# A hybrid attention layer on one core: probabilities scaled three slots ahead, a dilation-4 exchange by fixed 0/1 matrices and a pick, and loads in another order

## The chip, the cores and the metric

One Trainium2 chip, one of its cores. The metric is the device time of the whole kernel in microseconds, the median of several runs; lower is better.

## The reference

One decoder layer on x of 4096 tokens by 1024, in float32. The normed input goes through one projection whose columns feed three head groups; each group's output is gated by SiLU, all go through one output projection, are normed and added to x.

```python
qa, ka, va, ga, qb, kb, vb, gb, qc, gc = jnp.split(proj, IN_SPLITS, axis=-1)
oa, _ = banded_attention(qa * scale, ka, va, A_WINDOW - 1, sink)       # A: 6 heads, 2 key heads, window 128
for (win, dil) in ((128, 1), (512, 4), (2048, 16)):                    # B: 6 heads
    o, lse = banded_attention(to_strided(qb * scale, dil)[:, :, :, None, :],
                              to_strided(kb, dil), to_strided(vb, dil), win // dil, None)
    outs.append(from_strided(o[:, :, :, 0], B, dil)); lses.append(from_strided(lse[..., 0], B, dil))
wts = jax.nn.softmax(jnp.stack(lses, axis=0), axis=0)
ob = jnp.sum(wts[..., None] * jnp.stack(outs, axis=0), axis=0)
pc = jax.nn.softmax(jnp.einsum('bshd,bmhd->bhsm', qc * scale, mk), axis=-1)   # C: 4 heads, 256 memory tokens
y = jnp.concatenate([oa * silu(ga), ob * silu(gb), oc * silu(gc)], axis=-1)
h = h + rms_norm(jnp.einsum('bse,ed->bsd', y, w_out), post_norm)
```

## The kernel before

Three stages follow each other: `project_stage` (to about 1192 us of the profile), `attend_stage` (to about 2190) and `finish_stage`. The change is in the attention stage alone, in `head_group` and `attend_stage`.

**Units, slots and rounds.** The sequence is cut in two halves of 2048 tokens. A *phase* is one head on one half: 12 phases of group B, then 12 of A, then 8 of C. The work of a phase is a list of *units* (128 queries against 128 or 256 keys), 48 in B (16 for each dilation) and 16 in A and C, taken in pairs: `NP` is 24 or 8. In B the units come dilation 16 first, then in two groups with dilations 4 and 1.

The engines are driven by *rounds*. In round r the scores of phase r are made (`a`), while phase r-1 (`c`) is turned and multiplied with the values, and what is left of phase r-2 (`b`) is finished. A round has as many *slots* as the phase has pairs. `TAIL` says how many pairs of a phase are left for the round after the next: 8 in B, 2 in A and C. `slots_of` writes the table, so that the pair worked on in slot i of a round is `b`'s for i below the tail, then `c`'s.

Each slot does, on each engine in this order:

- **PE** (`tensor_round`): `scores` of the new pair (two products per unit, L952 and L953, since keys are held as a high and a low part), `turn` of the current pair's probabilities by transposing (L1017, into `ps_t`), `exchange`, and in every other slot `times_values` of two pairs (L1001). The scores have three PSUM buffers (`NS`).
- **DVE** (`vector_round`): `exchange`, `scale` of the pair of the next slot by its weight (L1135), `finish` of a bank of outputs (L1164 adds it to what was kept, L1169 multiplies by the gate), and the masked minimum of the scores, `scores` (L1048).
- **ACT** (`scalar_round`): `copy` of the turned pair to SBUF (L1207), `keep`, the exponentials with their sums (L1183), `exchange`.

**The exchange.** In B the minima and sums (`stat`) of the dilations 16 and 4 are held by strided queries and must be brought to the order of dilation 1, where the three are combined, and the weights (`work[:, 7]`) must go back. This is done by PE with 0/1 matrices: DVE first multiplies `stat` with a small 0/1 table `sel`, spreading it into `moved` (L1087 for dilation 16, 128 columns; L1090 for dilation 4, 512 columns), in slots 1 and 2. PE multiplies in slot 3 (L961, L965: `moved` as the stationary side, `sel` as the moving). DVE and ACT form the weights in slots 4 and 5 (L1096 to L1113), DVE spreads them (L1117, L1120), PE multiplies in slot 6 (L970, L972), and DVE copies them to `coef` in slot 7 (L1125).

**SyncE's queue.** `loads` issues all loads of a group, head after head, each behind the waits that free its buffer; a wait holds all that stands behind it:

```python
load_q(h, 0)                      # scores 8 slots into the phase before, and its queries copied
if not first: load_gate(h - 1, 1) # y_stored: output of two rounds ago stored
if new_keys: scored(*early_of, ...); load_k(h, 0)   # B: 13 slots into phase (h-1, 1)
if new_keys: scored(p1, NP, total); load_k(h, 1)
load_q(h, 1); load_gate(h, 0)
if new_keys: valued(*early_of, early); load_v(h, 0)
if new_keys: valued(p1, NP, total); load_v(h, 1)    # all values of phase (h-1, 1) done
```

In group A new keys and values come with heads 0 and 3 alone. **GpSimd** (`moves`) copies each phase's queries into two more orders (`spread_queries`, L601 four times and L609) once the phase before has its scores, and then issues the store of an output (L1228).

## Time and profile before

| | us |
|---|---|
| runs, median of 3 (2553.11 to 2563.31) | 2553.58 |
| profiled execution, its own time | 2546.56 |
| its span | 2545.1 |
| PE busy | 2283.6 (90%) |
| DVE busy | 1343.6 (53%) |
| ACT busy | 1141.8 (45%) |
| POOL busy | 134.5 (5%) |
| mean granted clock of TensorE | 0.947 |

The profiled execution is one run, 7.0 us below the median. Busy shares are over the whole span. A PE instruction counts as busy until its modelled end, so neighbours overlap. The clock is given as a share of 2.4 GHz; it is 1.0 or 0.5 at any time, and a mean between them tells how long it was at either. "L1017 <- DVE L1135" reads: the instruction of line 1017 waited, and that of line 1135 on DVE ended the wait.

### The profile page before, as it was taken

To read this page: it belongs to the slowest core of one execution; us is meant where nothing else is said; L and a number is where in the kernel's file an instruction comes from. 1 tells how busy PE (TensorE), PEld (TensorE's weight loads), DVE (VectorE), ACT (ScalarE), POOL (GpSimd) and SP (SyncE) were. 2 spreads that over 40 slices of the span, in tenths; PEclk is the share of its full clock that TensorE was granted. 3 is DMA by queue.
4 is the path that set the end of the run, shared out by engine and by line. 5 is a ranking of instruction groups with operands and counts; after the bars stand their busy time and mean duration, and the time that the engine had idled before them with its cause. 6 is when DMAs were issued, how large, how long until landed. Compare 5 with 4: busy or idle time off the path is not lost. (4 is left out here: it accounts for less than half of the span.)

```text
span 2545.1 us, 43938 instructions
## 1 busy us (share of the span) xinstructions
PE 2283.6 (90%) x13740; PEld 1912.2 (75%) x13740; DVE 1343.6 (53%) x3975; ACT 1141.8 (45%) x2967; POOL 134.5 (5%) x158
## 2 busy tenths in 40 slices
PE   5999999999999999998888798888877678799998
PEld 4887788877887788877777687776666567588887
DVE  4651347223751357212787777877787767333333
ACT  4123531245223532223777666765576667322221
POOL 0000000000000000010110101010121201000000
PEclk9999999999999999998799889998998889899999
DMA  5346334553345333474646737557368655344443
GB/s 183 136 165 165 129 112 148 176 146 117 132 172 162 129 124 141 138 213 114 113 83 134 142 67 149 107 110 143 84 137 177 147 144 154 120 149 148 142 139 114
DMA packets 349590, 350.27 MB, mean 138 GB/s; under 512 B 151568, under 2 KB 278160, under 8 KB 345360
## 3 DMA queue, kind: packets, MB, share of 16 engines
q1 hardware_dynamic: 341872, 322.54, 46.9%
q0 software_dynamic: 7584, 26.22, 4.1%
q8 instruction: 50, 0.82, 0.1%
q14 instruction: 84, 0.69, 0.1%
HBM read 222.07 MB, written 126.62 MB: 137 GB/s over the span
## 5 line engine op out<-in xcount | busy, mean ns | idle before, releaser
L58 PE MATMUL p_ps<-p_uT_hi,p_w_hi 128*128 128x512 f32 x1536 | 603.0, 393 | 2.1 <-DVE p_w_lo L389 2.1
L60 PE MATMUL p_ps<-p_uT_hi,p_w_lo 128*128 128x512 f32 x1536 | 599.4, 390 | 0.0
L59 PE MATMUL p_ps<-p_uT_lo,p_w_hi 128*128 128x512 f32 x1536 | 599.2, 390 | 0.0
L1183 ACT ACTIVATE probs<-probs,a_stat 128x256 f32<-128x256 f32 (+1 forms) x896 | 434.8, 492 | 107.3 <-DVE a_stat L1048 105.2
L952 PE MATMUL a_ps_s<-k_hi,q 128*128 128x256 f32 (+1 forms) x896 | 299.9, 352 | 98.5 <-DMA k_lo<-scratch_qk_lo 37.3
L1017 PE MATMUL a_ps_t<-a_ident,probs 128*128 128x128 f32 x1660 | 277.4, 291 | 70.5 <-DVE probs L1135 68.7
L58 PEld LDWEIGHTS p_ps<-p_uT_hi,p_w_hi 128*128 128x128 f32 x1536 | 289.4, 188 | 62.1 <-issue 2.5
L60 PEld LDWEIGHTS p_ps<-p_uT_hi,p_w_lo 128*128 128x128 f32 x1536 | 289.1, 188 | 60.9
L59 PEld LDWEIGHTS p_ps<-p_uT_lo,p_w_hi 128*128 128x128 f32 x1536 | 289.2, 188 | 59.0
L389 DVE TENSOR_TENSOR p_w_lo<-p_w_raw,p_w_hi 128x1024 fp32r<-128x1024 f32 x96 | 117.6, 1225 | 391.5 <-ACT p_w_hi L286 373.0
L1048 DVE CUSTOM_DVE_ANT_0 probs<-a_ps_s,a_maskB 128x256 f32<-128x256 f32 (+1 forms) x704 | 251.2, 395 | 134.0 <-PE a_ps_s L953 129.7
L1207 ACT ACTIVATE a_pT<-a_ps_t 128x512 f32<-128x512 f32 (+1 forms) x412 | 232.6, 567 | 193.7 <-PE a_ps_t L1017 193.4
L1135 DVE TENSOR_SCALAR probs<-probs,a_coef 128x256 f32<-128x256 f32 (+1 forms) x896 | 290.5, 369 | 26.8 <-issue 25.7
L952 PEld LDWEIGHTS a_ps_s<-k_hi,q 128*128 128x128 f32 x896 | 187.8, 210 | 142.9 <-issue 117.4
L1017 PEld LDWEIGHTS a_ps_t<-a_ident,probs 128*128 128x128 f32 x1660 | 204.1, 149 | 88.3 <-DVE probs L1135 81.8
L1001 PE MATMUL a_ps_o<-a_pT,a_v 128*64 128x128 f32 x3320 | 265.2, 301 | 2.9 <-ACT a_pT L1207 1.4
L953 PE MATMUL a_ps_s<-k_lo,q 128*128 128x256 f32 (+1 forms) x896 | 261.5, 308 | 0.0
L1001 PEld LDWEIGHTS a_ps_o<-a_pT,a_v 128*64 128x64 f32 x3320 | 199.9, 148 | 50.4 <-issue 31.7
L58 PE MATMUL f_ps<-f_w_hi,f_y_hi 128*128 128x512 f32 x512 | 200.3, 391 | 18.0 <-DVE f_w_lo L1538 18.0
L324 ACT ACTIVATE p_o_hi<-p_rot 128x512 fp32r<-128x512 f32 x80 | 50.6, 632 | 358.4 <-DVE p_rot L450 358.4
L59 PE MATMUL f_ps<-f_w_lo,f_y_hi 128*128 128x512 f32 x512 | 200.1, 391 | 0.0
L60 PE MATMUL f_ps<-f_w_hi,f_y_lo 128*128 128x512 f32 x512 | 200.0, 391 | 0.0
(113 smaller groups left out, 2371.6 us busy)
## 6 DMA issues: line engine op xcount, KB each, us to landing
p_w_raw<-in_w_in SPq DMA_DIRECT2D x96, 512.0 KB, 3.9
scratch_qk_hi<-p_o_hi SPq DMA_DIRECT2D x96, 256.0 KB, 2.0
scratch_qk_lo<-p_o_lo SPq DMA_DIRECT2D x96, 256.0 KB, 2.4
a_v<-scratch_v SPq DMA_DIRECT2D x40, 512.0 KB, 6.2
p_x<-in_x SPq DMA_DIRECT2D x32, 512.0 KB, 4.2
scratch_v<-p_o_v SPq DMA_DIRECT2D x256, 64.0 KB, 2.0
scratch_gate<-p_rot SPq DMA_DIRECT2D x64, 256.0 KB, 2.2
a_gate<-scratch_gate SPq DMA_DIRECT2D x64, 256.0 KB, 4.3
```

Of the source, the lines that this page charges most:

```text
L58: nc.tensor.matmul(out, w_hi, m_hi, start=first, stop=False)
L59: nc.tensor.matmul(out, w_hi, m_lo, start=False, stop=False)
L60: return nc.tensor.matmul(out, w_lo, m_hi, start=False, stop=last)
L389: nc.vector.tensor_tensor(w_lo[:, b, :, :].rearrange("p k n -> p (k n)"), w_raw[:, b, :], w_hi[:, b, :, :].rearrange("p k n -> p (k n)").b ...
L952: nc.tensor.matmul(out, w, keys_of(k_hi[:, 0:NKEY], u), start=True, stop=False)
L953: last = nc.tensor.matmul(out, w, keys_of(k_lo[:, 0:NKEY], u), start=False, stop=True)
L1001: last = nc.tensor.matmul(place_of(ps_o[j * HD:(j + 1) * HD, bank % 2, :], u), v[name][:, half, tile, :], pT[:, e % 4, j, at * P:(at + 1) ...
L1017: last = nc.tensor.transpose(ps_t[:, e % 2, j, at * P:(at + 1) * P], probs[:, s, 2 * e + j, at * P:(at + 1) * P], ident[:])
L1048: last = nc.vector.tensor_tensor_reduce(out=probs[:, s, 2 * slot + j, a:], in0=ps_s[:, slot % NS, j, a:], in1=masks[u.kind][:, a:], scale= ...
L1135: last = nc.vector.tensor_scalar(place, place, coef[:, s, u.column:u.column + 1], None, ALU.mult)
L1183: last = nc.scalar.activation(place, place, ACT.Exp, scale=-1.0, bias=stat[:, s, 0, u.column:u.column + 1], accum_out=stat[:, s, 1, u.colu ...
L1207: nc.scalar.activation(pT[:, e % 4, :, a[0]:], ps_t[:, e % 2, :, a[0]:], ACT.Copy).then_inc(turned_copied, 1)
```

## The change

1. `TAIL` goes from 8 to 12 in B and from 2 to 4 in A and C. DVE scales the pair that is turned three slots later. In a slot of DVE the order is now: exchange (A and C), scale, scores, finish, a new part `gated`, exchange (B). `gated` is the product with the gate, split off from `finish` and one slot later.
2. The dilation-4 part of the exchange has no spreading. `sel` holds, beside the small tables, four fixed 128x128 0/1 matrices `group4` (540 columns instead of 60). PE multiplies `stat` with them directly, 32 columns a product, four products instead of eight; DVE then picks from the result with a product with `col4` and a sum (into `picked` and back to PSUM). On the way back it is four products and the same pick. `moved` shrinks. The steps move: DVE in slots 1, 3, 5, 7, PE in slots 2 and 6, the end of a slot on DVE instead of its start.
3. `loads` is written out for all heads without a hardware loop, in another order. The second value load of a head now follows the next head's first query load and, in B, its first key load. In A and C the next head's first key load follows the gate load.
4. Group C's keys lie in the place of `v4`, its values in that of `v16`.
5. `start` of the score table at a switch of groups is max(0, lag - NP + 1) instead of 2.

GpSimd still copies the queries.

```diff
-    TAIL = 8 if kind == "B" else 2
+    TAIL = 12 if kind == "B" else 4
...
+    if kind == "C":
+        k_hi, k_lo = (buf.v["v4"][:, i, :, :].rearrange("p t n -> p (t n)")[:, 0:2 * NMEM].bitcast(F32R) for i in range(2))
+        v = {"v1": v["v16"]}
...
+        load_q(0, 0)
+        load_k(0, 0)
+        if prev:
+            load_mask()
+        for h in range(heads):
+            if new_keys(h):
                 load_k(h, 1)
-            if not prev and first:
-                load_v(h, 0)
+            if not prev and h == 0:
+                load_v(0, 0)
             load_q(h, 1)
             load_gate(h, 0)
-            if new_keys and (prev or not first):
-                valued(*early_of, early)
+            if new_keys(h) and (prev or h > 0):
                 load_v(h, 0)
-            if new_keys:
-                valued(p1, NP, total)
+            if h + 1 < heads:
+                load_q(h + 1, 0)
+            if new_keys(h + 1) and kind == "B":
+                load_k(h + 1, 0)
+            if new_keys(h):
                 load_v(h, 1)
+            load_gate(h, 1)
+            if new_keys(h + 1) and kind != "B":
+                load_k(h + 1, 0)
...
-            if kind == "B" and slot == 3:
-                pe.wait_ge(spread, 2 * p + 2)
+            if kind == "B" and slot == 2:
+                pe.wait_ge(spread, p + 1)
                 for x in range(2):
-                    nc.tensor.matmul(ps_x[:, 16 * x:16 * x + 16], moved[:, x, 0, :], col16,
-                                     start=True, stop=True)
-                    for c in range(NCH):
-                        at = 32 + 16 * x + 4 * c
-                        last = nc.tensor.matmul(ps_x[:, at:at + 4], moved[:, x, 1 + c, :], col4,
-                                                start=True, stop=True)
+                    nc.tensor.matmul(ps_x[:, 16 * x:16 * x + 16], moved[:, x, :], col16, start=True, stop=True)
+                for b in range(NCH):
+                    last = nc.tensor.matmul(ps_x[:, 128 + 32 * b:160 + 32 * b].rearrange("p (x n) -> p x n", x=2), group4[:, b, :],
+                                            stat[:, s, :, 16:32], start=True, stop=True)
                 last.then_inc(gathered, 1)
...
-            if slot == 4:
+            if slot == 1:
+                dve.wait_ge(sums_ready, p * NP + NP)
+                nc.vector.tensor_tensor(moved[:, 0:2, :].rearrange("p x (r a) -> p x r a", a=8),
+                                        stat[:, s, :, 0:16].unsqueeze(3).broadcast_to([P, 2, 16, 8]),
+                                        sel16.unsqueeze(1).unsqueeze(1).broadcast_to([P, 2, 16, 8]), ALU.mult).then_inc(spread, 1)
+            if slot == 3:
                 dve.wait_ge(gathered, p + 1)
+                own(nc.vector.tensor_tensor(picked[:, 0:128].rearrange("p (n r) -> p n r", r=NCH),
+                                            ps_x[:, 128:256].rearrange("p (n r) -> p n r", r=NCH),
+                                            col4.unsqueeze(1).broadcast_to([P, 32, NCH]), ALU.mult))
+                own(nc.vector.reduce_sum(ps_x[:, 32:64].rearrange("p (n b) -> p b n", b=NCH),
+                                         picked[:, 0:128].rearrange("p (b n r) -> p b n r", b=NCH, r=NCH),
+                                         mybir.AxisListType.X))
...
-            start = 2 if a and a.g is not c.g else 0
+            start = max(0, lag - a.g.NP + 1) if a and b and a.g is not b.g else 0
...
-                if c:
+                if c and c.g.kind != "B":
                     c.parts.exchange(c.phase, i)
-                if slot.next:
-                    x, e = slot.next
+                if slot.ahead:
+                    x, e = slot.ahead
                     x.parts.scale(x.phase, e)
+                for v in slot.new:
+                    a.parts.scores(a.phase, v)
                 if slot.two_before:
                     x, e = slot.two_before
                     x.parts.finish(x.phase, e)
-                for v in slot.new:
-                    a.parts.scores(a.phase, v)
+                if slot.three_before:
+                    x, e = slot.three_before
+                    x.parts.gated(x.phase, e)
+                if c and c.g.kind == "B":
+                    c.parts.exchange(c.phase, i)
```

**SyncE's queue in group B**, from the second value load of a head to the next head's first keys; before (the last value load ahead of the loop over heads, then the loop's first loads; `a_v` are the values, "ISA" carries a wait):

```order
L842 DMA a_v<-scratch_v 128x16x64 [waits B_values_done]
L842 DMA a_v<-scratch_v 128x16x64 x2
...
L812 DMA q<-scratch_qk_hi 64x2048
L813 DMA q<-scratch_qk_lo 64x2048
...
L854 DMA a_gate<-scratch_gate 64x16x64
...
L831 ISA [waits B_scores_ready]
L831 DMA k_hi<-scratch_qk_hi 64x16x128 x2
L831 DMA k_lo<-scratch_qk_lo 64x16x128 x2
```

And with the change, from a head's first value load to its second gate load:

```order
L855 DMA a_v<-scratch_v 128x16x64 [waits B_values_done]
L855 DMA a_v<-scratch_v 128x16x64 x2
L813 DMA q<-scratch_qk_hi 64x2048 [waits e_q_copied,B_scores_ready]
L814 DMA q<-scratch_qk_lo 64x2048
L839 DMA k_hi<-scratch_qk_hi 64x16x128 [waits B_scores_ready]
L839 DMA k_hi<-scratch_qk_hi 64x16x128
L839 DMA k_lo<-scratch_qk_lo 64x16x128 x2
L855 DMA a_v<-scratch_v 128x16x64 [waits B_values_done]
L855 DMA a_v<-scratch_v 128x16x64 x2
L863 DMA a_gate<-scratch_gate 64x16x64 [waits B_y_stored1]
L863 DMA a_gate<-scratch_gate 64x16x64
```

The keys stood behind both value loads, the queries and the gate; now they stand ahead of the second value load and of the gate.

**DVE in group B, slot 1 of an odd round, before** (L1087 and L1090 spread the minima, L1164 sums a bank):

```order
L1087 TENSOR_TENSOR a_moved<-a_stat,a_sel 128x128 [waits B_sums_ready]
L1090 TENSOR_TENSOR a_moved<-a_stat,a_sel 128x512
L1135 TENSOR_SCALAR probs<-probs,a_coef 128x256 x2
L1147 REGISTER_ALU
L1164 TENSOR_TENSOR probs<-a_ps_o,probs 64x2x128 [waits B_kept,B_y_ready,B_y_free_gate_loaded1,B_values_done]
L1164 TENSOR_TENSOR probs<-a_ps_o,probs 64x2x128 x3
L1168 REGISTER_ALU
L1169 TENSOR_TENSOR a_gate<-probs,a_gate 128x16x32 [waits B_bank_read]
```

**With the change, slot 5 of such a round** (L1025 is the minimum, L1141 the sum of a bank, L1079 the first step of the weights, L1091 the last; L1112 is the scaling of the next slot):

```order
L1025 ISA a_stat 128x1
...
L1141 TENSOR_TENSOR probs<-a_ps_o,probs 64x2x128 [waits B_kept,B_y_ready,B_y_free_gate_loaded1,B_values_done]
L1141 TENSOR_TENSOR probs<-a_ps_o,probs 64x2x128 x3
L1079 TENSOR_TENSOR a_work<-a_work,a_ps_s 128x32 [waits B_exps_ready]
L1081 TENSOR_TENSOR a_work<-a_work,a_stat 128x16
...
L1091 TENSOR_TENSOR a_moved<-a_work,a_sel 128x128 [waits B_shifted]
L1112 TENSOR_SCALAR probs<-probs,a_coef 128x256 x2
```

The exchange stood ahead of the slot's scaling; it is now the slot's last work, behind the minimum and, in slot 5, behind the sum of a bank. `B_spread_back` follows L1091.

**PE at the first exchange, before** (slot 3):

```order
L1017 MATMUL a_ps_t<-a_ident,probs 128x128 x3
L959 ISA
L961 MATMUL a_ps_s<-a_sel,a_moved 128x16 [waits B_spread]
L965 MATMUL a_ps_s<-a_sel,a_moved 128x4 x4
L961 MATMUL a_ps_s<-a_sel,a_moved 128x16
L965 MATMUL a_ps_s<-a_sel,a_moved 128x4 x4
```

**With the change** (slot 2; the line ahead is the turn of that slot):

```order
L994 MATMUL a_ps_t<-a_ident,probs 128x128 [waits B_turned_copied,B_weighted]
L994 MATMUL a_ps_t<-a_ident,probs 128x128 x3
L940 MATMUL a_ps_s<-a_sel,a_moved 128x16 [waits B_spread]
L940 MATMUL a_ps_s<-a_sel,a_moved 128x16
L942 MATMUL a_ps_s<-a_stat,a_sel 128x32 x4
```

Eight products of four columns became four of 32, one slot earlier.

## Rows read from the trace of the kernel before

**Rows 1.** The page: the span, then busy time and share of each engine
```profile
span 2545.1 us, 43938 instructions
...
PE 2283.6 (90%) x13740; PEld 1912.2 (75%) x13740; DVE 1343.6 (53%) x3975; ACT 1141.8 (45%) x2967; POOL 134.5 (5%) x158
```

**Rows 2.** Windows A:B: length, then busy us of PE, PEld, DVE, ACT, POOL; granted clock; DMA share; GB/s
```profile
40.00:1192.00 1152.00, 1111.82 (x5002) 913.48 (x5001) 462.00 (x694) 349.41 (x471) 11.85 (x15) 0.99 0.45 143
1255.00:1765.00 510.00, 437.82 (x3853) 377.86 (x3852) 392.35 (x1730) 355.56 (x1264) 60.66 (x71) 0.90 0.59 116
1765.00:1836.00 71.00, 57.79 (x522) 48.35 (x521) 46.80 (x169) 37.27 (x105) 7.07 (x6) 0.88 0.43 90
1836.00:2027.00 191.00, 138.82 (x1290) 119.10 (x1290) 142.78 (x536) 126.73 (x418) 35.98 (x34) 0.91 0.73 156
```

**Rows 3.** The same: group B's rounds 5 and 6, and a stretch of its round 1
```profile
1404.10:1458.60 54.50, 41.16 (x354) 34.60 (x352) 40.44 (x175) 37.25 (x135) 9.85 (x12) 0.90 0.78 147
1458.60:1507.30 48.70, 47.84 (x415) 42.20 (x415) 36.23 (x168) 33.32 (x117) 1.88 (x3) 0.83 0.38 76
1215.40:1235.90 20.50, 14.30 (x64) 13.70 (x64) 12.62 (x62) 11.36 (x46) 0.00 (x0) 0.50 0.13 31
```

**Rows 4.** Waits of PE, 1192 to 1765 us: us in total, times, longest
```profile
PE a_ps_t L1017 <- DVE probs L1135: 39.7, 35, 2.2
PE a_ps_s L952 <- DMA k_lo<-scratch_qk_lo: 23.8, 4, 6.7
...
PE a_ps_s L952 <- issue: 5.9, 1, 5.9
PE a_ps_s L961 <- DVE a_moved L1090: 5.2, 1, 5.2
PE a_ps_s L970 <- DVE a_moved L1120: 2.6, 1, 2.6
```

**Rows 5.** Timeline of SyncE's DMA issues in round 5 of B: start, length
```profile
1402.73 30.13 SPq L842 DMA_DIRECT2D a_v<-scratch_v  x6
...
1439.59 1.44 SPq L854 DMA_DIRECT2D a_gate<-scratch_gate  x2
1441.39 4.09 SPq L831 DMA_DIRECT2D k_hi<-scratch_qk_hi  x2
```

**Rows 6.** Timeline of DVE at the start of that round
```profile
1406.45 1.85 DVE L1087 TENSOR_TENSOR a_moved<-a_stat,a_sel 128x128 f32<-128x128 f32 x1
...
1409.35 1.72 DVE L1164 TENSOR_TENSOR probs<-a_ps_o,probs 64x256 f32<-64x256 f32 x4
```

**Rows 7.** Timeline of POOL in the same place
```profile
1403.91 2.40 POOL L601 CAST q<-q 128x512 fp32r<-128x512 f32 x4 [18.38 <-PE a_ps_s L953]
1406.26 1.89 POOL L609 CAST q<-q 128x2048 fp32r<-128x2048 f32 x1
```

**Rows 8.** Groups by line and shape, 1100 to 2250 us: busy, mean ns, idle before
```profile
L965 PE MATMUL a_ps_s<-a_sel,a_moved 128*128 128x4 f32 x192 | 29.4, 276 | 0.0
...
L1090 DVE TENSOR_TENSOR a_moved<-a_stat,a_sel 128x512 f32<-128x512 f32 x24 | 18.1, 753 | 0.0
...
L1087 DVE TENSOR_TENSOR a_moved<-a_stat,a_sel 128x128 f32<-128x128 f32 x24 | 14.7, 611 | 3.6 <-ACT probs L1183 3.6
```

**Rows 9.** Waits of PE in group A, 1836 to 2027 us
```profile
PE a_ps_t L1017 <- DVE probs L1135: 18.8, 13, 1.8
PE a_ps_s L952 <- DMA k_lo<-scratch_qk_lo: 13.4, 1, 13.4
PE a_ps_s L952 <- issue: 13.3, 1, 13.3
PE a_ps_s L952 <- POOL q L609: 9.0, 3, 4.6
```

**Rows 10.** Timeline of SyncE: the gate load ahead of A's second keys
```profile
1898.69 1.34 SPq L854 DMA_DIRECT2D a_gate<-scratch_gate  x2
```

**Rows 11.** Waits of PE in group C
```profile
PE a_ps_s L952 <- DMA k_lo<-scratch_mk_lo: 23.8, 3, 8.4
```

More of the change, by code:

```diff
@@ L969, in exchange @@
                 pe.wait_ge(spread_back, p + 1)
-                nc.tensor.matmul(ps_x[:, 64:80], moved_back[:, 0, :], col16, start=True, stop=True)
-                for c in range(NCH):
-                    last = nc.tensor.matmul(ps_x[:, 80 + 4 * c:84 + 4 * c], moved_back[:, 1 + c, :], col4,
+                nc.tensor.matmul(ps_x[:, 64:80], moved[:, 2, :], col16, start=True, stop=True)
+                for r in range(NCH):
+                    last = nc.tensor.matmul(ps_x[:, 256 + 16 * r:272 + 16 * r], group4[:, r, :], work[:, 7, 16:32],
                                             start=True, stop=True)
@@ L1312, in slots_of @@
             if not c:
-                return [named(new=[v], pair=None, before=None, two_before=None, next=None)
+                return [named(new=[v], pair=None, before=None, two_before=None, three_before=None, ahead=None)
                         for v in range(a.g.NP)]
```

138 lines of the change are left out of this document (54 added, 84 removed).

## The prediction, made before the kernel was run

> **What bounds the kernel now.** The page gives PE as busy for 90% of the span [rows 1], DVE for 53%; that is a mean over stages with different limits, so I read the windows by stage first. The projection stage (first row of [rows 2]) has PE busy for 1111.8 of 1152.0 us at a granted clock of 0.99: nothing that the diff touches could shorten it. Attention is the stretch with room. In 1255 to 1765 us, which is rounds 2 to 11 of head group B, PE is busy 437.8 of 510.0, DVE 392.4 and ACT 355.6, with the clock at 0.90. So ten rounds take 51.0 us each, no engine is full, and three engines each carry 36 to 44 us of every round. Such a stretch is bound by the waits among them, and by the clock.
>
> Next the same view for single rounds [rows 3]. Round 5 lasts 54.5 us with PE busy for 41.2; round 6 lasts 48.7 with PE busy for 47.8, but at a clock of 0.83. The odd round loses time in stands, the even one in half clock. A mean of 0.90 over 510 us means that a fifth of it ran at the lower level (1.2 instead of 2.4 GHz); were PE the bound all through, that would cost 0.10 x 510 = 51 us.
>
> The waits of PE [rows 4] then name the stands. There are two kinds: 39.7 us, 35 times, for DVE to scale the probabilities that PE transposes (L1017 waits for L1135), and 23.8 + 5.9 = 29.7 us, five times (the last is written "issue", at the switch to group A), for keys.
>
> Why are keys late? SyncE's queue shows it [rows 5]. In round 5 (from 1404.1) the six value loads stand ahead of everything. The second three of them waited for the values of the phase before the last, so that the row spans 30.1 us, to 1432.9. Then come the queries, the gate (1439.6), and only at 1441.4 the keys. PE starts on them at 1458.6 [rows 3]: 17.2 us after their first issue.
>
> Why is scaling late? DVE's timeline [rows 6]: one expansion of the exchange takes 1.85 us and the sum of a finished bank 1.72, both ahead of scaling that is done only one slot ahead of its use. The longest of PE's stands for it is 2.2 us [rows 4].
>
> **The change, part by part.** The sum is against the profiled execution, 2546.6 us (span 2545.1). It lies 7.0 us below the median of the runs, 2553.6; I add 7 at the end.
>
> *Keys of group B.* In the new queue the keys of the next head stand ahead of the second value load. They are released by slot 13 of 24 of an odd round: 13/24 x 43 us = 23 us into it, and 17.2 us more makes 40.5, inside a round of 42 to 43 us. Of the stands I take all: **-29.7**. The cover is thin: if a round shrinks below 40 us the keys bound it again. The value load that they pass is needed 12 slots into the next round, some 20 us later, so it costs nothing. The gate load moves behind both; its user is a finish at slot 5 of a later round, nothing again.
>
> *Scaling three slots ahead.* The turn of a pair then finds it scaled one or two slots earlier (a slot is 43/24 = 1.8 us), and the new order in a slot puts the minima before the sum of a bank. **-39.7** for the old stands. New ones appear. PE's exchange products now stand in slots 2 and 6, and each needs the work that DVE does last in the slot before. In slot 5 the sum of a bank, 1.72 us [rows 6], comes ahead of the exchange. For PE's stand there I bound 0 (no such stand in rounds 2 to 11) and 5.2 us (the longer of the two in round 1 [rows 4]); I take 2.0, near the 1.72 that is put in front. In slot 1 the GpSimd copies still run [rows 7]; the expansion under them took 1.85 us where its mean over all 24 is 0.61 [rows 8]. Between 0 and 1.85 I take 0.8. That is 2.8 x 10 rounds = **+28**.
>
> *Exchange.* Four of the eight dilation-4 products of the first step go. The 192 records of 29.4 us [rows 8] are 24 sets of four products (two records each), 1.2 us a set; of two sets a round one remains, with 32 columns instead of 4. I take 1.0 us a round: **-10**. The second step keeps its four products. On DVE the wide expansions of 0.75 us (L1090 twice [rows 8], and L1120, of the same size) go, three small products and sums come: some 1 us less a round. It is beside PE's work except in slots 1 and 5, where I have counted it.
>
> *Clock.* With keys and scaling on time the stands that precede the falls of the clock are gone, but the new ones at slots 2 and 6 are in their place. Of the 51 us I take two thirds, **-34**; the ends are 0 and -51.
>
> Rounds 2 to 11: -29.7 - 39.7 + 28 - 10 - 34 = **-85.4**, that is 42.5 us a round. PE's own need is (437.8 - 51)/10 = 38.7, DVE's 39.2, so 42.5 leaves each some 8% of slack, which is plausible for three engines coupled by double buffers.
>
> *The rest of attention.* Round 1: of 7.8 us at the exchange [rows 4] 5 go, as the wide expansions do: **-5**. Start: the constants table grows from 60 to 540 columns on the queue that PE waits for before its first scores: **+1**, by its size. Switch to A, 1765 to 1836 us: PE is idle for 13 us of that window [rows 2]; as it has no key load in it, I take 10 for stands for scaling, which go, and two more pairs with few scores beside them come: **-8**. Group A, 1836 to 2027: DVE is busy 142.8 of 191, PE 138.8. The 18.8 us of stands for scaling [rows 9] lie under DVE's own work, which keeps its order at slot 1: 0 for them. Of the 9.0 us for copied queries the longest, 4.6, comes from a query load behind a value load, which is now passed: **-4.6**. But the keys of A's second key head and C's first loads stand behind a gate load [rows 10], which needs the output of two rounds ago stored. With the tail at 4 slots instead of 2 that store comes two slots later; a slot of A is (191 - 27)/80 = 2 us (ten rounds of eight, less the two long stands), and this happens twice: **+8** on the 13.4 and 13.3. Group C: the same gate load still stands ahead of the keys; 23.8 us [rows 11] stay, as the store is two slots (3 us) later but no longer meets a query load. Its last round has two pairs more with nothing beside them: **+2.4**. Together: -5 + 1 - 8 - 4.6 + 8 + 2.4 = **-6.2**.
>
> Total: 2546.6 - 85.4 - 6.2 = 2455.0; with the 7 us to the median **2462**.
>
> **Two rules beside the rows.** The clock: [rows 3] show 0.83 in a round with under 1 us of idle PE that follows a 6.7 us stand, and 0.50 over 20.5 us in which PE was busy 14.3. The Trainium skill, "TensorE: Matmul & The Clock Gate", Part 1 and "HAM oscillation", says that the gate follows how busy the array has lately been, so that gaps are paid twice. By that rule alone, if the gaps vanish, all 51 us return and the sum is 2445. By the rows, gaps remain, hence two thirds.
>
> The copies: during the POOL copies the expansion took 1.85 us against a mean of 0.61 [rows 7, 8]. The Trainium skill, "SBUF — State Buffer", "Who interferes with whom", says that GpSimd and a DVE instruction with two SBUF inputs take the shared port pair in turn, the loser blocked for a whole instruction. This speaks against the change: the new expansion has two SBUF inputs, sits in slot 1 under the copies, and PE now waits for it one slot earlier.
>
> **The rivals.**
> - *Smoother*: DVE keeps ahead, as in the clean middle of a round, and PE never stands at slots 2 and 6. Then the 28 us are not paid and the clock returns in full (17 more): 2462 - 45 = **2417**. For it: no stand at the exchange in rounds 2 to 11 [rows 4]. Against: the bank's sum now ahead of it. 0.20.
> - *Copies at the exchange*: the copies of 2.40 + 1.89 us [rows 7] hold DVE up in slots 0 and 1; PE's stand in slot 2 grows by 2.7, to 3.5 us a round (+27), and the clock gives nothing back (+34): **2523**. 0.15.
> - *No gain*: the keys stay late, since another load of the queue (the first value load or the gate) waits longer with the tail of 12 slots, and new stands eat the rest: about **2550**. 0.05.
> - *Slower*: every round behaves like round 1 does now. There PE stands 5.2 + 2.6 us at the two exchanges and then has 20.5 us at half clock [rows 3, 4], 18 us in all. On 38.7 - 1 us of work that makes 56 us a round instead of 51: +50, with the +6 to +10 of the later stores some **2610**. It decides once PE's stands at slots 2 and 6 exceed about 7 us a round with the clock falling after each. In round 1 DVE is alone with the scores; later rounds gave PE other work in between. 0.04.
> - That the change doesn't do what it says: the order of instructions shows keys and scaling moved as told, so I give it nothing.
>
> **How the numbers follow.** The forecast has 0.56, with a range of its own of 2430 to 2495. With both neighbours the range 2412 to 2515 takes in the smoother case and the nearer part of the copies case, and leaves out the last two. About 0.5% (13 us) is what a measurement can tell from no change. Faster by more: 0.56 + 0.20 + 0.15 = 0.91; same 0.05; slower 0.04.
>
> **What would show it.** Right: the wait of PE for k_lo in group B gone; L1017's wait for scaling under 8 us in B; rounds of 41 to 44 us; a clock of 0.95 or more in B; waits of PE for the moved table at the first products of slots 2 and 6, 1 to 3 us a round; the 13 us stands in A and the 8 us ones in C still there or slightly longer. Wrong: a new wait for keys or values in B; a clock still at 0.90; stands at the exchange over 5 us; A rounds longer than 16.5 us because queries come late.

## The result, and the profile after

| | before | after |
|---|---|---|
| median of 20 runs each, us | 2554.39 | 2561.97 |
| lowest to highest | 2548.15 to 2563.80 | 2554.82 to 2567.41 |
| ratio, 95% interval | | 1.0025 (1.0015 to 1.0035) |
| profiled execution, own time (span), us | 2546.6 (2545.1) | 2561.1 (2559.3) |

The changed kernel is 0.25% slower, within the 0.5% that the prediction calls no change, and 100 us above the forecast of 2462, outside its range (to 2515). The change removed what it was to remove. The page, then the windows (length, busy us of PE, PEld, DVE, ACT, POOL; granted clock; DMA share; GB/s) of B's rounds 2 to 11, of A from its third round on, and of B's rounds 5 and 6 [rows 2, 3]:

```profile
span 2559.3 us, 43453 instructions
...
PE 2287.9 (89%) x13644; PEld 1919.2 (75%) x13644; DVE 1327.4 (52%) x3975; ACT 1143.4 (45%) x2967; POOL 134.5 (5%) x158
```
```profile
1250.10:1768.20 518.10, 443.98 (x3821) 384.98 (x3820) 378.46 (x1734) 361.16 (x1273) 60.65 (x71) 0.88 0.60 116
1832.70:2037.30 204.60, 143.87 (x1266) 124.78 (x1266) 142.73 (x530) 124.41 (x415) 35.91 (x33) 0.83 0.69 146
1401.40:1448.30 46.90, 40.10 (x352) 34.20 (x351) 38.43 (x171) 35.57 (x126) 5.76 (x7) 0.93 0.69 136
1448.30:1500.90 52.60, 46.07 (x402) 40.14 (x401) 35.47 (x172) 35.58 (x127) 5.92 (x8) 0.87 0.53 100
```

Round 5 fell from 54.5 us to 46.9, as the keys come in time; round 6 rose from 48.7 to 52.6, and the ten rounds from 51.0 us each to 51.8. The clock in them is 0.88, where it was 0.90 and 0.95 was expected. The waits of PE over B [rows 4] (total, times, longest):

```profile
PE a_ps_s L947 <- DVE a_moved L1091: 31.6, 11, 3.5
PE a_ps_o L978 <- ACT a_pT L1192: 15.3, 18, 1.9
PE a_ps_s L940 <- DVE a_moved L1059: 13.5, 8, 4.0
PE a_ps_t L994 <- ACT a_pT L1196: 10.0, 5, 3.5
PE a_ps_s L931 <- DMA a_maskB<-in_maskB: 9.3, 1, 9.3
PE a_ps_s L931 <- issue: 7.6, 1, 7.6
PE a_ps_t L994 <- DVE probs L1112: 2.4, 2, 1.7
```

L940 and L947 are the exchange's products of slots 2 and 6, L978 the product with the values, L994 the turn, L931 the scores. Keys (23.8 us) are gone from the list, and scaling is down from 39.7 us to 2.4. Four others fill it; the mask and the row written "issue", at the switch to A, were there before (9.2 and 5.9 us). In rounds 2 to 11 PE's idle time is 74.1 us, where it was 72.2.

**The stand in slot 6.** DVE's timeline of round 5 (start, length), and PE's product that waits for it:

```profile
1415.72 1.72 DVE L1141 TENSOR_TENSOR probs<-a_ps_o,probs 64x256 f32<-64x256 f32 x4
1417.47 0.19 DVE L1079 TENSOR_TENSOR a_work<-a_work,a_ps_s 128x32 f32<-128x32 f32 x1
...
1418.02 0.25 DVE L1084 RECIPROCAL a_work<-a_work 128x16 f32<-128x16 f32 x1
...
1418.62 0.29 DVE L1091 TENSOR_TENSOR a_moved<-a_work,a_sel 128x128 f32<-128x128 f32 x1
```
```profile
1418.96 0.28 PE L947 MATMUL a_ps_s<-a_sel,a_moved 128*128 128x16 f32 x1 [2.83 <-DVE a_moved L1091]
```

The bank's sum (1.72 us) stands first, as predicted, and behind it the seven small steps of the weights, 1.44 us from 1417.47 to 1418.91. The prediction priced the sum and left the steps out.

**The stand in slot 2.** DVE and POOL at the start of the same round [rows 6, 7]:

```profile
1401.95 1.22 DVE L1112 TENSOR_SCALAR probs<-probs,a_coef 128x256 f32<-128x256 f32 x2
...
1403.77 2.12 DVE L1112 TENSOR_SCALAR probs<-probs,a_coef 128x256 f32<-128x256 f32 x2
...
1406.50 0.41 DVE L1059 TENSOR_TENSOR a_moved<-a_stat,a_sel 128x256 f32<-128x256 f32 x1
1406.84 0.60 DVE L1112 TENSOR_SCALAR probs<-probs,a_coef 128x256 f32<-128x256 f32 x2
```
```profile
1401.23 2.41 POOL L601 CAST q<-q 128x512 fp32r<-128x512 f32 x4 [10.09 <-PE a_ps_s L932]
1403.59 1.90 POOL L609 CAST q<-q 128x2048 fp32r<-128x2048 f32 x1
```

While GpSimd copies, two pairs of scalings take 1.22 and 2.12 us; the pair after the copies takes 0.60. Before, the same large copy lay over the expansion (1.85 us, [rows 6]). So the price moved from one operation to another: the new expansion takes 0.41 us in all 12 phases, but comes 2.1 us late (0.6 and 1.5 us over the usual 0.60). This is so in rounds 2, 3, 5, 7, 9 and 11, the same six in which an expansion was slow before; in rounds 4, 6, 8 and 10 no scaling is slowed. The Trainium skill, "SBUF — State Buffer", "Who interferes with whom", says that a tensor_scalar, too, can enter a mode that takes the port pair shared with GpSimd, and that whoever issues second is then blocked until the other's instruction ends. These rows agree: the copy lasts 1.90 us, and the slowed pair takes 2.12.

**The stand at the turn of the loop.** B's heads 1 to 5 are a hardware loop, and at the start of rounds 4, 6, 8 and 10 it turns. There DVE stops without a wait that the profile shows: in the waits of DVE of the kernel before, then of the one after, and of ACT after:

```profile
DVE probs L1135 <- issue: 25.7, 4, 7.0
```
```profile
DVE probs L1112 <- issue: 17.8, 4, 4.9
```
```profile
ACT a_pT L1195 <- issue: 13.1, 4, 4.0
```

Before, PE stood for keys in the same places, 5.5 to 6.7 us, so this stop had a cover. Now the keys are early and it lies bare: PE's stands there are 1.8 to 3.5 us. Round 8, on DVE, ACT and PE:

```profile
1555.18 0.62 DVE L1112 TENSOR_SCALAR probs<-probs,a_coef 128x256 f32<-128x256 f32 x2 [4.89 <-issue]
```
```profile
1555.81 0.28 ACT L1195 ACTIVATE a_pT<-a_ps_t 128x128 f32<-128x128 f32 x1 [3.67 <-issue]
```
```profile
1556.50 0.87 PE L994 MATMUL a_ps_t<-a_ident,probs 128*128 128x128 f32 x3 [3.19 <-ACT a_pT L1196]
```

**The clock.** "Behind a stand" means here: beginning during it or within 3 us of its end. Three stretches behind a stand, at the loop's turn (round 6), behind a stand of 2.72 us in slot 6 (round 4) and behind one of 2.83 (round 5):

```profile
1454.10:1464.30 10.20, 9.41 (x49) 8.41 (x51) 5.42 (x33) 5.33 (x22) 0.00 (x0) 0.50 1.06 194
1372.10:1375.50 3.40, 3.40 (x24) 3.07 (x20) 1.38 (x10) 0.52 (x3) 0.00 (x0) 0.51 0.00 0
1419.90:1423.30 3.40, 3.40 (x25) 3.03 (x25) 1.35 (x5) 1.09 (x4) 0.00 (x0) 0.50 0.00 0
```

PE is full in the last two and runs at the lower level. Summed over the clock's record, the half-clock stretches that begin in rounds 2 to 11 were 105.8 us long before and are 133.1 now; the last of them runs past the end of round 11, and cut there the sums are 101.8 and 119.3. Of the 17 stands of 0.6 us and more before the exchange's first products in slots 2 and 6, 16 have such a stretch behind them, 82 us in all (one of them, of 10.2 us in round 4, lies behind the stand at the loop's turn as well). Half clock costs up to half its length: within these rounds about 9 us more than before, instead of 34 less.

**Group A.** The waits of PE there, and GpSimd in one round [rows 9]:

```profile
PE a_ps_s L931 <- POOL q L609: 21.1, 8, 2.9
PE a_ps_s L931 <- DMA k_lo<-scratch_qk_lo: 19.5, 1, 19.5
```
```profile
1862.96 1.67 POOL L1213 DMA_DIRECT2D scratch_y<-a_gate  x2 [13.33 <-DVE a_gate L1146]
1864.62 1.90 POOL L609 CAST q<-q 128x2048 fp32r<-128x2048 f32 x1
```

The longer tail makes the output later, GpSimd waits for it before it issues the store, and the last copy of the next queries stands behind the store. Eight of A's rounds now wait 2.5 to 2.9 us for queries, and behind each of the eight stands the clock is at half for 3.4 us: the mean over A is 0.83, where it was 0.91. The two stands behind a gate load [rows 10] went from 13.4 and 13.3 us to 19.5 and, at the switch to C, 20.1.

### The profile page after: what moved, and what is told of

It reads as the page before. It is cut to its first block and busy times, and to the rows that moved or that the text cites. A ratio compares the mean times of both kernels' runs of the same rounds, so it can differ in the third digit from the quotient of the medians.

```text
span 2559.3 us, 43453 instructions
## 1 busy us (share of the span) xinstructions
PE 2287.9 (89%) x13644; PEld 1919.2 (75%) x13644; DVE 1327.4 (52%) x3975; ACT 1143.4 (45%) x2967; POOL 134.5 (5%) x158
## 3 DMA queue, kind: packets, MB, share of 16 engines
q1 hardware_dynamic: 341872, 322.78, 46.9%
## 5 line engine op out<-in xcount | busy, mean ns | idle before, releaser
L1025 DVE CUSTOM_DVE_ANT_0 probs<-a_ps_s,a_maskB 128x256 f32<-128x256 f32 (+1 forms) x704 | 251.2, 395 | 207.2 <-PE a_ps_s L932 201.2
L389 DVE TENSOR_TENSOR p_w_lo<-p_w_raw,p_w_hi 128x1024 fp32r<-128x1024 f32 x96 | 117.6, 1225 | 392.2 <-ACT p_w_hi L286 373.7
L931 PE MATMUL a_ps_s<-k_hi,q 128*128 128x256 f32 (+1 forms) x768 | 260.9, 356 | 64.2 <-POOL q L609 27.5
L1112 DVE TENSOR_SCALAR probs<-probs,a_coef 128x256 f32<-128x256 f32 (+1 forms) x896 | 295.3, 375 | 18.9 <-issue 17.8
L978 PE MATMUL a_ps_o<-a_pT,a_v 128*64 128x128 f32 x3320 | 273.7, 304 | 20.1 <-ACT a_pT L1192 17.5
L994 PE MATMUL a_ps_t<-a_ident,probs 128*128 128x128 f32 x1660 | 278.8, 293 | 13.2 <-ACT a_pT L1196 10.0
L978 PEld LDWEIGHTS a_ps_o<-a_pT,a_v 128*64 128x64 f32 x3320 | 203.4, 150 | 70.7 <-ACT a_pT L1192 33.7
L931 PEld LDWEIGHTS a_ps_s<-k_hi,q 128*128 128x128 f32 x768 | 164.4, 214 | 103.5 <-issue 85.2
L932 PE MATMUL a_ps_s<-k_lo,q 128*128 128x256 f32 (+1 forms) x768 | 228.9, 313 | 0.0
L994 PEld LDWEIGHTS a_ps_t<-a_ident,probs 128*128 128x128 f32 x1660 | 211.5, 151 | 18.8 <-DVE probs L1112 14.1
```

Of the source, the lines that this page charges most:

```text
L389: nc.vector.tensor_tensor(w_lo[:, b, :, :].rearrange("p k n -> p (k n)"), w_raw[:, b, :], w_hi[:, b, :, :].rearrange("p k n -> p (k n)").b ...
L931: nc.tensor.matmul(out, w, keys_of(k_hi[:, 0:NKEY], u), start=True, stop=False)
L932: last = nc.tensor.matmul(out, w, keys_of(k_lo[:, 0:NKEY], u), start=False, stop=True)
L978: last = nc.tensor.matmul(place_of(ps_o[j * HD:(j + 1) * HD, bank % 2, :], u), v[name][:, half, tile, :], pT[:, e % 4, j, at * P:(at + 1) ...
L994: last = nc.tensor.transpose(ps_t[:, e % 2, j, at * P:(at + 1) * P], probs[:, s, 2 * e + j, at * P:(at + 1) * P], ident[:])
L1025: last = nc.vector.tensor_tensor_reduce(out=probs[:, s, 2 * slot + j, a:], in0=ps_s[:, slot % NS, j, a:], in1=masks[u.kind][:, a:], scale= ...
```

## The experiments

Each is timed against the kernel before on one chip, not all of them on the same one; hence the spread of the first row. "B", "A" are rounds 2 to 11 of the group, from its profile, and "C" is that group's eight rounds, to the end of its scores. "half" is the length of the half-clock stretches that begin in B's rounds, the last one in full (up to 14 us of it lie behind round 11); "idle" is PE's idle time in B.

| version | median us | ratio (95%) | B | half | idle | A | C |
|---|---|---|---|---|---|---|---|
| before | 2553 to 2559 | | 509.7 | 105.8 | 72.2 | 190.8 | 128.4 |
| after | 2561.97 | 1.0025 | 518.1 | 133.1 | 74.1 | 204.7 | 133.6 |
| x1_loads | 2534.69 | 0.9920 (.9888–.9951) | 506.8 | 109.2 | 66.3 | 188.6 | 117.6 |
| x2_unroll | 2546.43 | 0.9963 (.9949–.9978) | 509.4 | 146.8 | 62.7 | 204.5 | 132.1 |
| x3_before_unroll | 2549.79 | 0.9971 (.9954–.9988) | 510.7 | 116.1 | 72.5 | 192.7 | 129.4 |
| x4_shift | 2535.39 | 0.9907 (.9880–.9934) | 499.7 | 105.8 | 65.3 | 204.4 | 132.3 |
| x5_pool | 2563.38 | 1.0033 (1.0017–1.0049) | 518.7 | 143.4 | 72.1 | 214.8 | 133.7 |
| x6_gates | 2512.80 | 0.9841 (.9810–.9872) | 511.6 | 122.9 | 66.2 | 179.4 | 123.0 |
| x8_all | 2471.29 | 0.9668 (.9638–.9698) | 468.1 | 64.9 | 46.0 | 189.5 | 121.1 |
| x9_exchange | 2520.58 | 0.9873 (.9847–.9899) | 490.9 | 85.3 | 72.6 | 191.5 | 127.8 |
| x10_both | 2497.06 | 0.9775 (.9740–.9809) | 478.3 | 58.0 | 66.4 | 189.3 | 116.6 |
| x12_one_ahead | 2568.86 | 1.0059 (1.0038–1.0079) | 518.3 | 136.5 | 71.6 | 204.5 | 133.2 |
| x13_ac_old | 2541.25 | 0.9949 (.9924–.9973) | 520.9 | 143.4 | 73.7 | 197.1 | 125.2 |
| x14_all_ac_old | 2445.69 | 0.9582 (.9552–.9613) | 460.7 | 58.0 | 44.3 | 177.1 | 105.9 |
| x16_tail12 | 2500.52 | 0.9767 (.9749–.9784) | 489.6 | 81.9 | 63.5 | 189.3 | 118.3 |
| x17_later | 2419.59 | 0.9443 (.9418–.9467) | 439.0 | 27.3 | 36.0 | 174.7 | 108.4 |
| x11_best | 2442.06 | 0.9543 (.9527–.9559) | 462.4 | 58.0 | 47.1 | 170.1 | 104.2 |
| x18_moved | 2514.21 | 0.9833 (.9808–.9859) | 475.2 | 71.7 | 55.9 | 204.6 | 132.4 |

### One part on the kernel before

x1_loads puts the change's `loads`, written out, and C's new places into the kernel before.

```diff
+        for h in range(heads):
...
+            if new_keys(h + 1) and kind == "B":
+                load_k(h + 1, 0)
+            if new_keys(h):
                 load_v(h, 1)
-        head(0, True)
```

> The kernel before with the new order of loads alone (and group C's keys and values in their new places); tails, scaling and exchange as before. Theory 'code': at each turn of the loop over heads DVE and ACT stop 4 to 7 us for code, at the same place where PE stands for keys (rounds 4, 6, 8, 10), so keys that come early uncover that stop: 2540 to 2552, the even rounds keep a stand of 3 to 5 us, only the two key stands without a loop turn (rounds 2's end and the switch to A) shrink. Rival 'keys' (the prediction's term): all 29.7 us go, 2520 to 2528.

2534.7 us, between the two ranges, but B gained only 3 us; C gave 11, which neither had. In the place of the waits for keys PE now waits 47.2 us for scaling and 15.8 us, in three stands, for nothing that the profile shows. At the four turns of the loop it stands 4.3, 4.9, 3.4 and 4.5 us, where it stood 5.5 to 6.7 for keys: the stop of DVE lies bare here too. Early keys alone are not worth their 29.7 us.

x9_exchange takes the new exchange alone into the kernel before, in its old slots, tail 8, one ahead. Set beside the changed kernel's exchange (not the kernel before), its steps differ by this, and PE's first product is in slot 3:

```diff
-            if slot == 3:
+            if slot == 4:
...
-            n = [p * DVE_STEPS + {3: 0, 5: 4, 7: 7}.get(slot, 0)]
+            n = [p * DVE_STEPS + {4: 0, 5: 4, 7: 7}.get(slot, 0)]
```

> The kernel before with the new exchange alone (fixed matrices and pick), in its old slots and its old place in a slot, tail of 8. The prediction's term: 1 us a round of PE and 1 us of DVE, 12 rounds, and shorter stands for scaling behind the spreading in slots 1 and 2: 2530 to 2545. Rival: the longer chain on DVE (a pick is two dependent steps) makes DVE the later one: 2555 to 2565.

2520.6 us, better than forecast, B down by 19. x10_both joins the two.

> The kernel before with the two parts that were each faster alone: the new exchange in its old slots (-32 us alone) and the new order of loads with group C's new places (-19 us alone). Tails (8/2), scaling one slot ahead and the slots of the exchange stay as before. Theory (the loss sits in the longer tail and what goes with it: three slots ahead, moved slots): the parts add up, about 2500 us (-2%), rounds 2 to 11 of B together near 488 us, against 518 in the changed kernel. Rival (the loss comes from early keys meeting the new exchange, since the stop of DVE at a turn of the loop then lies bare): rounds 2 to 11 near 505 us or more, 2520 us or more in all, and a stand of 3 us with half clock behind it at the start of rounds 4, 6, 8, 10.

2497.1 us, the parts add up, and B is shorter than the theory had it. So two of the change's parts are worth 2.2% together, and what is left of it costs 65 us: the tails, three ahead, the new order within a slot of DVE, and the moved steps. The window of rounds 2 to 11 and PE's waits in it:

```profile
1246.50:1724.80 478.30, 411.91 (x3772) 353.72 (x3771) 381.49 (x1727) 354.11 (x1264) 60.93 (x71) 0.94 0.65 125
```
```profile
PE a_ps_t L994 <- DVE probs L1112: 56.3, 38, 4.0
PE a_ps_s L931 <- issue: 6.6, 1, 6.6
```

PE is idle here for 66.4 us, nearly as long as in the changed kernel (74.1), and most of it, 56.3 us, waits for scaling (14.3 of them at the loop's turns); yet the clock is 0.94. Of its 31 stands for scaling of 0.6 us and more 13 have half clock behind them, 51 us; in the changed kernel 16 of 17 at the exchange had, and 22 of all its 31 of that length. What differs between 478 and 518 us is 8 us of idle time, and 65 us of half clock within the rounds, some 33 us of time.

### Which of the remaining parts costs it

x12_one_ahead is the changed kernel scaling one slot ahead.

```diff
-two_before=pair(i - 2), three_before=pair(i - 3), ahead=pair(i + 3))
+two_before=pair(i - 2), three_before=pair(i - 3), ahead=pair(i + 1))
```

> The changed kernel with probabilities scaled one slot ahead instead of three; tails stay 12 and 4, everything else stays. Theory (three ahead does what it says: turns no longer wait for scaling): the waits of the turning for the scaling come back, 30 to 40 us of them in B and some 15 in A, and the kernel takes 2585 us or more. Rival (three ahead only moves work of DVE in front of the exchange and buys nothing, since the turning would have its pairs anyway): the stands at the moved tables shrink, and the time is 2562 us or less.

```profile
PE a_ps_t L994 <- DVE probs L1112: 31.4, 30, 3.6
PE a_ps_s L947 <- DVE a_moved L1091: 29.2, 10, 3.1
...
PE a_ps_s L940 <- DVE a_moved L1059: 1.8, 5, 0.4
```

Between the two. The scaling waits come back, 31.4 us as the theory had it, but B stays at 518.3. 12.1 us of them are the stands at the turn of the loop, which were written to ACT (10.0 us, now 0.6) and have not gone. Against the other 19.3 us, the waits for L1059 (9.5 to 1.8 us) and for ACT at L978 (14.7 to 0.5) go. Three ahead swaps stands nearly one for one; of its 7 us, 5 lie behind C's last scores.

x16_tail12 raises B's tail in x10_both to 12, with the `start` that it needs.

```diff
-    TAIL = 8 if kind == "B" else 2
+    TAIL = 12 if kind == "B" else 2
```

> The version with the new exchange in its old slots and the new loads (2497 us), with the tail of B raised from 8 to 12 and nothing else in B; scaling is one slot ahead, A and C keep tail 2. Theory (the moved steps of the exchange cost the 40 us, since their short stands split the work of TensorE and each is followed by a stretch at half clock): rounds 2 to 11 of B stay within 8 us of 478, half clock under 80 us, the kernel near 2497 us. Rival (the tail of 12 brings DVE's bank sums and gate products into the slots of the exchange): rounds 2 to 11 at 500 us or more, the kernel at 2520 us or more.

2500.5 us against 2497.1: B is 11 us longer, three more than the theory allowed, and the switch to A 10 us shorter. The tail explains a quarter of the 40 us inside these rounds and nothing of the total.

x4_shift puts each step of the exchange one slot later in the changed kernel; x18_moved puts PE's second product two later.

```diff
-            if kind == "B" and slot == 2:
+            if kind == "B" and slot == 3:
...
-            if kind == "B" and slot == 6:
+            if kind == "B" and slot == 8:
...
-            n = [p * DVE_STEPS + {3: 0, 5: 4, 7: 7}.get(slot, 0)]
+            n = [p * DVE_STEPS + {4: 0, 6: 4, 8: 7}.get(slot, 0)]
```

(x4_shift has 7 in place of 8 on PE; ACT's step goes from slot 4 to 5 in both.)

> The changed kernel with PE's exchange products one slot later (3 and 7 instead of 2 and 6) and DVE's and ACT's steps behind them one slot later (DVE 4, 6, 8, ACT 5). Theory 'exchange': PE's stands for the moved table, 1.5 and 2.8 us a round, go, and with them most of the 3.4 to 6.8 us at half clock behind each: 2500 to 2520. Rival 'work': DVE's work is the bound and PE stands elsewhere for it: 2550 to 2562.

> The changed kernel with nothing but the steps of its exchange placed later: TensorE's products in slots 3 and 8 instead of 2 and 6, DVE's steps in slots 4, 6 and 8 instead of 3, 5 and 7, ACT's in 5 instead of 4. Theory (the places of the two products cost the 40 us, 8 us of them as idle time and the rest as half clock): rounds 2 to 11 of B come to 478 to 485 us from 518, half clock from 133 to below 80 us, the kernel near 2525 us. Rival (part of the 40 us belongs to the stop at the loop's turn, which this version keeps bare): rounds 2 to 11 at 490 to 500 us, 2535 us or more, no better than the version with both products one slot later, 2535 us.

```profile
1247.90:1723.10 475.20, 419.32 (x3821) 362.44 (x3820) 379.04 (x1734) 361.47 (x1272) 60.75 (x71) 0.93 0.65 126
```
```profile
PE a_ps_s L947 <- DVE a_moved L1091: 19.8, 10, 2.4
PE a_ps_o L978 <- ACT a_pT L1192: 15.5, 15, 1.9
PE a_ps_s L931 <- issue: 7.7, 1, 7.7
PE a_ps_t L994 <- ACT a_pT L1196: 7.0, 5, 2.6
```

x4_shift removed the stand for L1059 and left that for L1091 (28.4 us); x18_moved cut the latter to 19.8 us. B fell by 18 and by 43 us. x4_shift gave less than its theory (2500 to 2520), as the stand in slot 6 stayed; x18_moved gave more. Everything else of the change stayed in this version, so the places of the exchange's steps make the 40 us of B: 18 us as idle time, and 52 us of half clock within the rounds, which is up to 26 us of time.

### The loop, the queues, and group A

x2_unroll and x3_before_unroll write B's rounds out, in the changed kernel and in the one before.

```diff
-                with eng.Fori(1, g.heads) as h:
...
+                    for h in range(1, g.heads):
+                        pair_of_rounds(h)
```

> The changed kernel with group B's rounds written out instead of a hardware loop on PE, DVE and ACT. Theory 'code': the stands of about 3 us after slot 2 of rounds 4, 6, 8, 10 and the 10 us at half clock that follow them go: 4 x (3.2 + 3 to 5), 2530 to 2540. Rival 'work' (DVE and ACT are full, stops only shift): 2555 to 2562. If code comes late without a loop as well: slower than 2562.

> The kernel before with group B's rounds written out. Theory 'code': DVE's four stops (25.7 us) go, but PE still stands for keys at the same place, so little is won: 2545 to 2555. Rival: if the stops themselves delay the keys (through the scores that release them), 2530.

In x2_unroll DVE's waits have no issue row any more, idle time fell by 11 us and the kernel by 15.5. That is less than forecast: half clock grew (146.8 us against 133.1) where the theory had it shrink, so B fell by 8.7. In the kernel before B did not move (510.7 against 509.7), though DVE's issue row is gone there too: PE stood for keys all the same. The stop is real and its cost depends on its cover. The Trainium skill, "Runtime: NRT & Kernel Launch", "Instruction fetch mechanics", says that a branch taken out of what is loaded stops an engine until its code is fetched. These runs agree with it and give a size, 4.1 to 7.0 us on DVE.

x5_pool lets GpSimd copy the next queries ahead of the store in A.

```diff
+            for h in range(1, heads):
+                copy_queries(pool, h, 1)
+                store(pool, h - 1, 0)
+                if h + 1 < heads:
+                    copy_queries(pool, h + 1, 0)
+                store(pool, h - 1, 1)
```

> The changed kernel; in group A GpSimd copies the queries of a phase ahead of the store of the phase three before, instead of behind it. Theory 'store': ten of A's rounds wait 2.6 us for copied queries because the store ahead of the copy comes two slots later with a tail of four; these waits go and the rounds shrink from 17.0 to about 15.5 us, DVE's work: 2543 to 2552. Rival: the queries' loads are late, not the copy: same as the changed kernel, 2560.

2563.4 us, a miss; it came out as the rival had it. A's rounds took 16.5 to 20.2 us, the stands before keys 22.3 and 21.6, and PE waits for queries as long as before:

```profile
PE a_ps_s L931 <- POOL q L609: 21.7, 8, 4.7
```
```profile
1847.62 1.34 SPq L863 DMA_DIRECT2D a_gate<-scratch_gate  x2
1849.01 0.97 SPq L813 DMA_DIRECT2D q<-scratch_qk_hi  x1
```
```profile
1857.44 1.90 POOL L609 CAST q<-q 128x2048 fp32r<-128x2048 f32 x1 [13.27 <-issue]
```

The copy no longer stands behind a store, but the load of the queries stands behind a gate load, and that one waits for a store. So the copy's place is not the whole cause: copy and load both hang on the late output. x13_ac_old takes that away and returns A and C to tail 2, one ahead.

```diff
-    TAIL = 12 if kind == "B" else 4
+    TAIL = 12 if kind == "B" else 2
...
+                far, near = pair(i + 3), pair(i + 1)
+                if far and far[0].g.kind == "B":
+                    return far
+                return near if near and near[0].g.kind != "B" else None
```

> The changed kernel with group B as it is, but A and C as in the kernel before: tail 2 and scaling one slot ahead. Theory (tail 4 puts A's stores later, so that GpSimd issues a store late and copies the next queries late): the wait of PE for the queries in A, 2.6 us a round, goes, A's rounds are 15.5 to 16.3 us again, waits for scaling of about 1 us a round come back; A rounds 2 to 11 near 191 us against 205, the kernel near 2548 us. Rival (the wait for the queries is set by the loads and the gates ahead of them): A stays above 200 us and the kernel within 5 us of 2562.

2541.3 us, and the wait for queries in those rounds of A is one of 1.0 us: the tail of four, with the scaling three ahead that goes back with it here, is its cause. Waits for scaling (18.2 us) come back, so that A is 197.1 us, and not 191. x6_gates puts the next head's keys ahead of the second gate load in A and C, and the group's last gate load behind the next group's first loads.

```diff
-            if new_keys(h + 1) and kind == "B":
+            if new_keys(h + 1):
                 load_k(h + 1, 0)
...
-            load_gate(h, 1)
-            if new_keys(h + 1) and kind != "B":
-                load_k(h + 1, 0)
+            if h + 1 < heads or kind == "C":
+                load_gate(h, 1)
```

> The changed kernel with the next head's first key load ahead of the second gate load in A and C as well, and the last gate load of a group behind the next group's first loads. Theory 'gate': the stands of 19.5 and 20.1 us in A and 8.9, 8.6, 8.8 in C come from keys behind a gate load that waits for a store; they shrink to under 5 in all: 2495 to 2515. Rival 'queries': queries or copies are as late as the keys, so half stays: 2535.

2512.8 us, 49 less: 25 of them in A, 11 in C and 6.5 in B, where the stand at the switch to A goes. The stand in A's round 5 fell from 19.5 to 7.6 us and that of 20.1 at the switch to C is gone (one of 10.3 for queries follows it).

### Together

x8_all has x2, x4, x5 and x6 in one, x14_all_ac_old has x13's A and C in place of x5. x11_best writes B out and moves the gates in x10_both. x17_later is x14_all_ac_old with PE's second product in slot 8.

> The changed kernel with the loop of group B written out, the exchange one slot later, GpSimd's copies ahead of stores in A, and keys ahead of gates. If the parts add: -15 (written out) -27 (later exchange) -12 (copies) -50 (gates), about 2458; if the stands hide one another, 2480 to 2500.

> The kernel with everything that helped: B's rounds written out, its exchange one slot later, keys ahead of the second gate load, and A and C with tail 2 and scaling one slot ahead; copies and stores of GpSimd in their old order. The kernel with the first three and with the other order of copy and store took 2471 us. Theory (the tail of A and C costs 10 us or more, and the other order of copy and store gave nothing): 2455 to 2465 us. Rival (with keys ahead of the gates A no longer waits for queries, so the tail is free there): 2470 us or more.

> The version with the new exchange in its old slots, tail 8, one ahead and the new loads (2497 us), with B's rounds written out and the keys ahead of the second gate load. Theory (both mends are worth here what they were worth in the changed kernel, 15 and 49 us, less what the new loads with tail 2 already gave in C): 2440 to 2455 us, level with the 2446 us of tail 12. Rival (with tail 8 the scaling waits, 56 us in B, keep the loop's stop hidden, so that writing out gives nothing): 2460 us or more.

> The fastest version so far (2446 us: B written out, exchange one slot later, keys ahead of gates, A and C as before) with TensorE's second product of the exchange one slot later still, in slot 8, and DVE's pick at the end of the same slot. Theory (the stand before the second product, 2.2 to 3.1 us a round, is a matter of place: DVE has spread the weights one slot later): the stand goes, with the half clock behind it, about -30 us of B, the kernel near 2420 us. Rival (the stand moves: DVE's pick then waits for the product, what DVE has queued behind it comes late, and the turning or the scores stand in its place): 2440 us or more.

2471.3, 2445.7, 2442.1 and 2419.6 us: the first between its two forecasts, the second better than its theory, the other two as theirs had it. The last is 5.6% faster than the kernel before, and the fastest here:

```profile
1247.60:1686.70 439.10, 403.12 (x3822) 348.19 (x3820) 387.13 (x1734) 358.21 (x1272) 61.66 (x71) 0.97 0.69 136
```
```profile
PE a_ps_s L950 <- DVE a_moved L1094: 17.7, 10, 2.2
PE a_ps_o L981 <- ACT a_pT L1195: 14.7, 18, 1.8
```

Its rounds are 43.9 us, near the 42.5 forecast for the change. The stand did not go, as its theory had it; it fell from 26.8 to 17.7 us, and half clock from 58.0 to 27.3.

## Why the prediction was wrong

By stage the profiled executions differ by +14.2 us (spans); the medians differ by 7.6, as the profiled execution before is 7.8 us below its median. Outside B's rounds 2 to 11 the sum was 12 us off, ten of them in A: start and round 1 -4 forecast, -4.8 found; switch to A -8 and -7.1; A +3.4 and +13.9; C +2.4 and +5.2, with some 1.4 less behind it. The miss of 94 us in rounds 2 to 11 (-85.4 forecast, +8.4 found) falls into these steps:

- **Keys, -29.7: failed.** The loads came in time (1430.6 us in round 5, 18 us before its end, [rows 5]) and the wait for k_lo went. But "Of the stands I take all" overlooked what stood under them, the stop of DVE and ACT at the loop's turn. It was in the trace before, 25.7 us in four. PE stands 10.0 + 1.7 us there now; at the switch to A, where the keys were as late as ever, 7.6 us instead of 5.9. By the stands that are left the term was worth -10. x1, x2 and x3 show the cover.
- **Scaling three ahead, -39.7: the stands went, as told.** But x12 shows that B is as long without it: the work put ahead on DVE came back as stands elsewhere.
- **Stands at the exchange, +28: mis-sized, 38.0 measured.** The slot-6 stand was 2.85 us a round against 2.0, as the chain of weights behind the bank's sum was left out. The slot-2 one was 0.95 against 0.8, and its cause was not a slow expansion but slowed scalings ahead of it. To these come 16.3 us for ACT's copies at L978 (2.7 before), which no step foresaw.
- **Exchange products, -10: right for what it priced, but not the whole.** The first step's dilation-4 products went from 29.4 to 17.5 us of busy time, 1.0 us a round. The exchange's other products took longer, 26.1 us against 20.9 from 1250 to 1770 us (those of the second step have 16 columns instead of 4); all of them together fell from 45.6 to 41.7 us there.
- **Clock, -34: failed, about +9.** This is nearly half of the miss. The prediction had the new stands "in their place" and still let two thirds return. In the kernel before, 12 of 25 stands for scaling of 0.6 us and more had half clock behind them; at the exchange it is 16 of 17. Ten of those 17 last 2.7 to 3.5 us, longer than any stand for scaling before (2.2), so length may be a part of it; but of the seven of 1.0 to 1.5 us six have it too. x10 and x18 against the changed kernel show the price.
- **A, +3.4: 13.9 measured.** The store's delay was priced for the gates (+8 against 12.9, with the one at the switch), and not for the queries, which hang on the same store by GpSimd's copy and, as x5 shows, by their load as well; x13 shows that they come in time without the longer tail. The 18.8 us of stands for scaling, taken to stay, went; queries and half clock came in their place.

Of the rivals, *No gain* (2550) came nearest in time, but for another reason: no load of B stayed late. The mechanism of *Slower*, a stand at the exchange with half clock behind it, is what took place, at 3.8 us a round instead of the 7 from which it was to decide. Its chance was too low because one stand and one half-clock stretch were priced apart, and because every stand removed was booked as time. Two of the prediction's own signs of being wrong appeared: a clock no better than 0.90 in B (0.88), and rounds of A over 16.5 us because queries come late (17.0).

## What to carry to other kernels

Before a wait is booked as gain, list what else stands still in the same microseconds: a stop under it comes to light when it goes. When steps of a chain are moved closer together, price the whole chain that must end first, not its longest member, and give the moved wait its half clock too. And where a load or store is made later, follow everything behind it on its queue: the order of key and gate loads was worth 49 us here.

## What the runs showed of the hardware

- DVE stops for 4.1 to 7.0 us where a hardware loop of two rounds turns (25.7 us in four before, 17.8 after), and ACT in the changed kernel for up to 4.0 (13.1 in four), with no wait shown; written out, the stop is gone.
- Equal idle time does not give an equal clock: within rounds 2 to 11, 66.4 us of idle with 54 us at half clock in x10_both, 71.6 with 122 in x12_one_ahead. Of the seven stands of 1.0 to 1.5 us before the exchange's products in the changed kernel six had half clock behind them; of the 14 stands of 1.3 to 1.5 us for scaling in x10_both three had. Of the changed kernel's five stands of 1.87 us at L978 two had, and every stand of 2.5 us and more. Why a short stand counts in one place and not in another was not tested.
- Under a GpSimd copy of 1.9 us a scaling took up to 1.98 us, where its median is 0.35. The copies were left where they are in every version, so what they cost in all was not tried.
